# Rows in eight phases over 1024-row macro tiles, with the 31-tap convolution as block-Toeplitz matmuls

## The reference

```
mod = silu(c) @ w_ada + b_ada;  shift, scale, gate = split(mod, 3)
h = rmsnorm(x, norm_g) * (1 + scale) + shift
a_in, a_b, a_c, a_z, b_v, b_g, b_z = split(h @ w_in)          # 7 blocks of 512 columns
y_a = a_b * dwconv3(a_c * a_in) * silu(a_z)
u = dwconv31(b_v * sigmoid(b_g)) + conv_b_b
y_b = silu(head_layernorm(u, ln_g, ln_b)) * silu(b_z)         # norm over each head's 64 channels
x = x + gate * (concat([y_a, y_b]) @ w_out);  out = rmsnorm(x, final_g)
```

## Time and profile before

| | |
|---|---|
| time, median of 3 runs | 2577.07 us (2572.67 to 2577.63) |
| span of the profiled execution (slowest core) | 2570.0 us; all cores 2563.3 to 2570.0 |
| TensorE | busy 94% of the span |
| VectorE, ScalarE, GpSimd | busy 48%, 48%, 30% |
| DMA | 283 MB, 110 GB/s |
| TensorE's granted clock | 0.99 of full speed |

### The profile page before, as it was taken

The page is one execution under the profiler, slowest core; times in us unless marked ns, Lnnn a source line. Parts: engine busy times, 40 slices in busy tenths (PEclk is TensorE's granted clock), DMA queues, the critical chain, the costliest instruction groups (busy, mean ns, idle before and its releaser), DMA issues.

```text
span 2570.0 us, 46749 instructions; the slowest of 8 cores (2563.3 to 2570.0 us)
## 1 busy us (share of the span) xinstructions
PE 2428.4 (94%) x14724; PEld 1074.0 (42%) x14724; DVE 1245.8 (48%) x1972; ACT 1231.0 (48%) x2054; POOL 781.0 (30%) x838
## 2 busy tenths in 40 slices
PE   5799999999999999999999999999999999999995
PEld 1334444444444444444444444444444444444432
DVE  1234454545454545454545455455455455445455
ACT  1144555544555554455554455554454554455544
POOL 3113333223323223323323323323323323333314
PEclk9899999999999999999999999999999999999998
DMA  9954223344322344322334322344422334432232
GB/s 220 200 134 125 87 81 92 117 125 125 96 80 91 109 125 125 107 78 83 109 125 133 118 70 88 101 133 125 125 82 82 102 118 125 125 94 80 61 110 99
DMA packets 89914, 283.05 MB, mean 110 GB/s; under 512 B 15016, under 2 KB 24400, under 8 KB 89680
## 3 DMA queue, kind: packets, MB, share of 16 engines
q1 hardware_dynamic: 80176, 270.64, 35.0%
q0 software_dynamic: 9504, 9.44, 2.7%
HBM read 168.96 MB, written 67.13 MB: 92 GB/s over the span
## 4 chain that ended last, share of the span: by engine, by line
PE 70%; ACT 15%; issue 6%; POOL 3%; DMA 3%; DVE 2%; another core or an unknown queue 0%; ACTq 0%; SPq 0%; POOLq 0%; DVEq 0%
PE pb L446 50%; PE pb L646 12%; PE pb L575 6%; ACT L605 3%; ACT L609 3%; ACT tp L607 3%; POOL yT L619 2%; ACT tp L615 2%; DMA w_in_sb<-w_in 2%; PE pb L586 1%; ACT tp L608 1%; ACT gb L553 1%; ACT sq L580 1%; ACT tp L465 1%; DVE tp L563 0%
## 5 line engine op out<-in xcount | busy, mean ns | idle before, releaser
L446 PE MATMUL pb<-hT,w_in_sb 128*128 128x512 bf16 x7168 | 1594.7, 381 | 18.7 <-DMA w_in_sb<-w_in 16.7
L446 PEld LDWEIGHTS pb<-hT,w_in_sb 128*128 128x128 bf16 x7168 | 699.4, 98 | 860.8 <-issue 50.8
L646 PE MATMUL pb<-w_out_sb,yT 128*128 128x512 bf16 x2048 | 470.7, 380 | 17.4 <-POOL yT L619 16.6
L465 ACT ACTIVATE tp<-pb 128x512 f32<-128x512 f32 x384 | 225.1, 595 | 488.5 <-PE pb L446 487.8
L619 POOL TENSOR_TENSOR yT<-tp,gb 128x512 bf16<-128x512 f32 x128 | 145.1, 1155 | 862.1 <-ACT tp L615 862.1
L658 POOL TENSOR_TENSOR xb<-tp,xb 128x512 f32<-128x512 f32 x256 | 321.7, 1267 | 142.0 <-DVE tp L656 123.8
L693 ACT ACTIVATE tp<-xb 128x1024 bf16<-128x1024 f32 x128 | 135.3, 1057 | 428.9 <-POOL xb L658 428.9
L646 PEld LDWEIGHTS pb<-w_out_sb,yT 128*128 128x128 bf16 x2048 | 195.5, 98 | 247.6 <-issue 37.5
L703 DVE SCALAR_TENSOR_TENSOR xb<-xb,rsE,fg_bc 128x1024 f32<-128x1024 f32 x128 | 164.4, 1284 | 227.1 <-POOL rsE L701 227.1
L575 PE MATMUL pb<-V,WC 128*32 128x512 bf16 x4096 | 244.4, 381 | 0.0
L656 DVE TENSOR_TENSOR tp<-pb,gate_bc 128x512 f32<-128x512 f32 x256 | 173.7, 689 | 121.5 <-PE pb L646 109.8
(11 more groups left out here) (74 smaller groups left out, 1503.7 us busy)
## 6 DMA issues: line engine op xcount, KB each, us to landing
xb<-x SPq DMA_DIRECT2D x256, 512.0 KB, 6.4
y<-xb SPq DMA_DIRECT2D x128, 512.0 KB, 2.7
V<-u SPq DMA_DIRECT2D x128, 135.9 KB, 2.6
V<-u SPq DMA_DIRECT2D x128, 135.8 KB, 2.6
V<-u SPq DMA_DIRECT2D x128, 135.6 KB, 2.7
xb<-w_ada SPq DMA_DIRECT2D x24, 512.0 KB, 9.7
w_in_sb<-w_in POOLq DMA_DIRECT2D x14, 512.0 KB, 28.3
gate_bc<-gate_scratch SPq DMA_DIRECT2D x5, 512.0 KB, 7.2
```

The source lines that it names most:

```text
L446: T.op("tensor", lambda e, bank=bank, kc=kc: e.matmul(bank[:], lhsT=w_in_sb[:, kc, col0:col0 + 128], rhs=hT[:, kc, :], start=(kc == 0), st ...
L465: T.op("scalar", lambda e: e.activation(out=t[:], in_=bank[:], func=func, scale=scale), reads=[bkey], writes=[tkey])
L646: T.op("tensor", lambda e, kc=kc: e.matmul(bank[:], lhsT=yT[:, kc, sub * 128:(sub + 1) * 128], rhs=w_out_sb[:, kc, h * NT:(h + 1) * NT], s ...
```

## The change

A macro tile is 1024 consecutive rows, 16 per core. Its rows are dealt into eight phases r = 0 to 7: row 8n + r is column n of phase r. A tile is now half a macro tile: four phases of 128 rows each (q = 0 or 1), so that x is loaded and y stored with a stride of eight rows.

- **Convolution.** `V` now has 16 channels by 8 phases on the partitions and the index n on the free axis, 32 groups of 16 channels. `u` reaches it through a scratch tensor in HBM: `u_store` (4 transfers per tile, 131 KB, runs of 256 bytes) and `v_load` (4 per macro tile, 262 KB, runs of 256 bytes). One group's 31 taps are five matmuls of 128 by 128 with a block-Toeplitz matrix `wc` (SH = 5 shifts of n); the output has rows on the partitions and (phase, channel) on the free axis. A macro tile needs 8 `conv` of 20 matmuls with 128 columns each. The Toeplitz matrices are built at the start (`wc_build`, 8 instructions of 128x2560 and 8 stores of 655 KB) and are loaded again for each macro tile, 655 KB per `conv`, into a ring of two buffers (`wc_load`).
- **Head norm.** The 64 channels of a head now lie on the free axis: VectorE adds the bias and sums them (`s1`, `s2`, `s4`), ScalarE squares (`s3`), GpSimd takes the power and multiplies (`s4`, `s5`). The steps are handed out one per `tick()`, which each projection group and each `conv` calls. The result is turned back by a crossbar DMA on SP (`s6`, 262 KB, 4 per macro tile), then ScalarE's Silu and a VectorE multiply into `gb` (`fin_half`). No Ln or Exp is left.
- **Norm of x.** The 32 TensorE transposes per tile go away (except for tile 0): `xbar` turns `xs` by crossbar DMA, 4 of 262 KB per tile, and ScalarE applies the modulation in place in one of two `hT` buffers (`h_mod`, 8 per tile). The scaling moves from GpSimd to ScalarE.
- **Seams.** The rows right of each macro tile that isn't its sequence's last (11 times 16 rows) are projected once at the start (`halo_pairs`, 128 matmuls with 176 columns). PSUM is now one ring of 8 banks instead of 6 and 2; the ring of x buffers has 6 instead of 8.

```diff
-UW = 544
-TAP0 = (0, 1, 8, 9, 16, 17, 24, 25)
+PH = 8
+MT = 1024
+SH = 5
...
-        V = sb("V", [128, 4, 4, UW], BF16)
...
+        WC = Ring("wc", [sb("wc%d" % i, [128, 4 * SH * 128], BF16) for i in range(2)], T)
+        V = sb("V", [128, 32, 132], BF16)
...
+        def xbar(i, sub):
+            hT = hTb[i % 2]
+            T.dma("sync", lambda e: e.dma_start_transpose(out=hT[:, :, sub * 128:(sub + 1) * 128], in_=xs[:, sub, :]),
+                  reads=[("xs", sub)], writes=[("hTs", i % 2, sub)], semkey=("xt", i % 2, sub))
...
+        def h_mod(i, kc, eng="scalar"):
+            hT, s = hTb[i % 2], mac_seq[i // 2]
+            r, w = [("hTs", i % 2, sub) for sub in range(4)] + ["gsT", "shT"], [("hT", i % 2, kc)]
+            if eng == "scalar":
+                T.op("scalar", lambda e: e.activation(out=hT[:, kc, :], in_=hT[:, kc, :], func=AF.Identity, scale=gsT[:, kc, s:s + 1],
+                                                      bias=shT[:, kc, s:s + 1]), reads=r, writes=w)
...
+        def wc_load(h):
+            w, wkey = WC.next(pin=True)
+            T.dma("sync", lambda e: e.dma_start(out=w[:], in_=wc_d[h]), reads=[("wcd", h)], writes=[wkey], semkey=("wcl", wkey[1]))
+            wc_slot[h] = (w, wkey)
...
+        def u_store(i, j):
+            m, q = divmod(i, 2)
+            T.dma("sync", lambda e: e.dma_start(out=u_d[m % 2, j * 128:(j + 1) * 128, 4 * q:4 * q + 4, :],
+                                                in_=u_sb[:, j, :].rearrange("p (s n) -> p s n", s=4)),
+                  reads=[("u", j)], writes=[("ud", m % 2, q, j)], semkey=("us", q, j))
...
+        def v_load(m, j):
+            T.dma("sync", lambda e: e.dma_start(out=V[:, 8 * j:8 * j + 8, 2:130],
+                                                in_=u_d[m % 2, j * 128:(j + 1) * 128].rearrange("(g c) s n -> (c s) g n", c=16)),
+                  reads=[("ud", m % 2, 0, j), ("ud", m % 2, 1, j)], writes=[("V", j)], semkey=("vl", j))
...
+        def tick():
+            for st_ in list(lnq):
+                if st_[0]() is None:
+                    st_.pop(0)
+                if not st_:
+                    lnq.remove(st_)
...
+        def conv(m, h):
+            tick()
+            j = h // 2
+            bank, bkey = PB.next(pin=True)
+            w, wkey = wc_slot.pop(h)
+            for g in range(4):
+                for k in range(SH):
+                    T.op("tensor", lambda e, g=g, k=k: e.matmul(
+                        bank[:, g * 128:(g + 1) * 128], lhsT=V[:, 4 * h + g, k:k + 128], rhs=w[:, (g * SH + k) * 128:(g * SH + k + 1) * 128],
+                        start=(k == 0), stop=(k == SH - 1)),
+                        reads=[wkey, ("V", j), "Vl", "Vr"], writes=[bkey], signal=(g == 3 and k == SH - 1))
+            WC.unpin(wkey)
...
+            def s1():
+                T.op("vector", lambda e: e.tensor_tensor(out=o4, in0=bank[:].rearrange("p (g r c) -> p r g c", g=4, r=PH), in1=cb, op=ALU.add),
+                     reads=[bkey, "cbb"], writes=[okey])
+                PB.unpin(bkey)
+
+            def s2():
+                T.op("vector", lambda e: e.reduce_sum(out=ls[:, 0, :], in_=o3, axis=mybir.AxisListType.X), reads=[okey], writes=[lskey])
+                T.op("vector", lambda e: e.tensor_scalar(out=ls[:, 1, :], in0=ls[:, 0, :], scalar1=1.0 / 64, scalar2=None, op0=ALU.mult),
+                     reads=[lskey], writes=[lskey])
+                T.op("vector", lambda e: e.tensor_tensor(out=o3, in0=o3, in1=bc(1), op=ALU.subtract), reads=[okey, lskey], writes=[okey])
+
+            def s3():
+                sq[0], sqkey[0] = SQ.next(pin=True)
+                T.op("scalar", lambda e: e.activation(out=sq[0][:], in_=o[:], func=AF.Square), reads=[okey], writes=[sqkey[0]])
+
+            def s4():
+                T.op("vector", lambda e: e.reduce_sum(out=ls[:, 2, :], in_=sq[0][:].rearrange("p (r c) -> p r c", r=PH), axis=mybir.AxisListType.X),
+                     reads=[sqkey[0], lskey], writes=[lskey])
+                SQ.unpin(sqkey[0])
+                T.op("vector", lambda e: e.tensor_scalar(out=ls[:, 2, :], in0=ls[:, 2, :], scalar1=1.0 / 64, scalar2=LN_EPS, op0=ALU.mult, op1=ALU.add),
+                     reads=[lskey], writes=[lskey])
+                T.op("gpsimd", lambda e: e.tensor_tensor(out=ls[:, 3, :], in0=ls[:, 2, :], in1=mhalf[:], op=ALU.pow),
+                     reads=[lskey, "mhalf"], writes=[lskey])
+
+            def s5():
+                T.op("gpsimd", lambda e: e.tensor_tensor(out=xn[:, :, (h % 2) * 64:(h % 2) * 64 + 64], in0=o3, in1=bc(3), op=ALU.mult),
+                     reads=[okey, lskey], writes=[(xnkey, h % 2)] + ([xnkey] if h % 2 == 0 else []))
+                TP.unpin(okey)
+                LS.unpin(lskey)
+
...
+                def s6():
+                    if len(BR.pinned) == len(BR.bufs):
+                        return False
+                    got.extend(BR.next(pin=True))
+                    br, brkey = got
+                    T.dma("sync", lambda e: e.dma_start_transpose(out=br[:], in_=xn[:].rearrange("p r c -> p (r c)")),
+                          reads=[xnkey, (xnkey, 0), (xnkey, 1)], writes=[brkey], semkey=("yt", brkey[1]))
+                    XN.unpin(xnkey)
+                    return None
+
+                def fin_half(q):
+                    def f():
+                        if (m, q, j) not in zdone:
+                            return False
+                        br, brkey = got
+                        tt, ttkey = TP.next()
+                        T.op("scalar", lambda e: e.activation(out=tt[:], in_=br[:, 4 * q:4 * q + 4, :].rearrange("p r n -> p (r n)"), func=AF.Silu,
+                                                              scale=lng[:, j:j + 1], bias=lnb[:, j:j + 1]),
+                             reads=[brkey, "lng", "lnb"], writes=[ttkey])
+                        gv = gb[:, j, 4 * q:4 * q + 4, :].rearrange("p r n -> p (r n)")
+                        T.op("vector", lambda e: e.tensor_tensor(out=gv, in0=gv, in1=tt[:], op=ALU.mult),
+                             reads=[ttkey, ("gb", j, q)], writes=[("gb", j, q)])
+                        if q == 1:
...
+                steps += [s6, lambda: None, fin_half(0), fin_half(1)]
+            steps[0]()
+            lnq.append(steps[1:])
...
-        def conv_b(j):
-            bank, bkey = PB.next(pin=True)
-            for p in range(8):
-                for g in range(4):
-                    T.op("tensor", lambda e, p=p, g=g: e.matmul(
-                        bank[32 * g:32 * g + 32, :], lhsT=WC[:, (j * 4 + g) * 8 + p, :], rhs=V[:, g, j, TAP0[p]:TAP0[p] + NT],
-                        start=(p == 0), stop=(p == 7), tile_position=(0, 32 * g)),
-                        reads=[("WC", j)] + [("V", k, g) for k in range(4)], writes=[bkey], signal=(p == 7 and g == 3))
...
-        def conv_mean(j):
-            bank, bkey, vv, vkey = cst[j]
-            T.op("tensor", lambda e: e.matmul(bank[:], lhsT=Bn[:], rhs=vv[:], start=False, stop=True, skip_group_check=True),
...
+        for h in range(8):
+            wc_build(h)
+        pair_all("a2", 0)
+        for n in range(6):
+            a_next(1, n)
         for j in range(4):
             zb(0, j)
...
+        for kc in range(8):
+            h_mod(1, kc, "vector" if kc % 2 else "scalar")
...
+            if q == 1:
+                wc_load(0)
+                wc_load(1)
+                v_left(m)
...
+                    a_next(nxt, j)
+                if q == 1 and j:
+                    v_load(m, j - 1)
...
+            if pm >= 0:
+                out_proj(pm, q, conv_in=m if last else None)
...
+            if q == 0:
+                work = [lambda j=j: pair("a2", i, j) for j in range(4)] + [lambda j=j: zb(i, j) for j in range(4)]
+                for n, f in enumerate(work):
+                    f()
+                    if pm >= 0 and n < 4:
+                        conv_a(1, n)
+                    if fin and n in (0, 1):
+                        d_finish()
+                    if nxt is not None:
+                        h_mod(nxt, n)
+            else:
+                work = [f for j in range(4) for f in (lambda j=j: pair("a2", i, j), lambda j=j: zb(i, j))]
+                for n, f in enumerate(work):
+                    f()
+                    if fin and n in (0, 1):
+                        d_finish()
+                    if not last:
+                        conv(m, n)
+                        if n < 6:
+                            wc_load(n + 2)
+                    if nxt is not None:
+                        h_mod(nxt, n)
```

782 lines of the change are left out of this document (399 added, 383 removed).

## The result

The changed kernel takes 2648.37 us (median of 5 runs) against 2577.07, ratio **1.026** (95% interval 1.023 to 1.028): slower by 2.6%, where 2425 was forecast, and above the range's end of 2620. The profiled execution spans 2633.9 us.

What follows compares the result with a forecast made beforehand. TensorE's program order was taken as the bound: 126 + 35 + 10 + 2090 (its matmuls) + 113 + 14 + 15 + 15 = 2418 us of span, 2425 as median with 7 us added. Range of 8 in 10: 2285 to 2620 us.

Steps and rivals of the forecast that it cites:

- the a2 product of group 0 ends near 4.4 us into the stage: Start of the stage with conv: VectorE's a2 product ends at 4.4 us, and the first norm turn is issued at 19.
- two last norms with their waits 4.3: VectorE in the stage with conv: two last norms of output rows, 4.3 us, ahead of the first turn.
- the term of +7.5 us for the stage: Stage with conv: `conv` 7 ends at 37.2 instead of 29.7 us, in each of 15 macro tiles, 113 us.
- `conv` 7: Last conv of the stage: its weight load stands behind the second turn on SP, so it begins at 36.1 us.
- the loop: Norm in the stage with conv: turn, Silu, product, variance, power and GpSimd product lead to the next turn, 10.6 us.
- the next tile's last `h_mod`: Tile seam: it follows zb's own 0.6 us on ScalarE, +0.5 us at each of 31 seams, 15 in all.
- Short matmuls, reduction, power: Prices per instruction: 0.056 us per 128-column matmul on TensorE, 0.68 per VectorE reduction, 1.7 per GpSimd power.
- Rival D: TensorE's short matmuls take 97 ns each because weight loads aren't hidden, total 2530 us; chance 0.09.
- X + 6.6: Time from one norm turn to the next: X, the crossbar transfer, taken as 4 us, plus 6.6 us of other steps.
- rival C: Crossbar turns keep the 16 DMA engines busy, making the kernel slower; 2700 us at 8 us per turn; chance 0.21.
- The start: Before the steady part: +35 us for stores and the build of `wc`, +10 for tile 2's loads behind the gate.
- The end: From the last matmul to the kernel's end: stays at 15 us.

Runs made afterwards that it cites:

- f2: The change with the first half tile's 3-tap convolutions moved from ahead of out_proj to the next tile's glu phase, all work kept: 2602.52 us.
- f1: The change without the final norm of output rows finished in stages with conv, and with the Silu halves two slots later; work left out: 2495.51 us.
- e1: The change with y stores issued behind the conv weight loads of h=2 and 3 in SyncE's order, same work: 2630.94 us.
- e3: The change without the conv weight loads of h=2 to 7 in every stage; output not the reference's: 2646.71 us.
- e7: The change without the weight loads of h=2 to 7, with Silu halves two slots later and the output finish cut in two: 2605.56 us.
- f7: The change with 3-tap convolutions moved, Silu halves later, start and end reordered and y stores later, all work kept: 2529.56 us, ratio 0.981 to the kernel before.
- e5: The change with the two Silu halves of a turned norm output two slots later in ScalarE's order, same work: 2595.16 us.
- e9: The change with the last three row finishes of a stage with conv moved behind groups 1, 3 and 5, same work: 2698.21 us.
- e2: The change with all conv weight loads issued from ScalarE's queue instead of SyncE's, same work: 2706.45 us.

## Why the prediction was wrong

The span is 2633.9 instead of 2418: 216 us. From the trace, the first stage starts at 237.2, where the sum had 126 + 45 + 27.6 of matmuls + 5 = 203.6: 34 us. The 14 macro tiles from there take 2121.3 us, where 14 x 141.9 = 1986.6 were forecast: **135 us**, 9.6 each. The rest, to the end, takes 275.4 instead of 228: 48 us.

- **The step that failed** is "the a2 product of group 0 ends near 4.4 us into the stage", and with it "two last norms with their waits 4.3". I let VectorE and ScalarE enter the stage without backlog. The product ends 9.9 us in, and four last norms stand in the stage, with 8.8 us of waits. The first turn is issued at 25.1, not at 19. In the sum this is the term of +7.5 us for the stage: up to the next tile's eighth matmul the forecast is 29.7 + 7.5 + 0.5 + 1.5 (seven matmuls) = 39.2 us, and 47.8 were measured. Where no row finish stands in the stage, the first turn is at 18.9 and the stage lasts 41.0 (first stage of f2), or 18.6 and 39.0 (f1). That these come near the forecast is in part chance: the forecast held two last norms and these stages none, and their a2 product still ends 2.5 to 2.7 us after the forecast's.
- **What is late next** was named in part. For `conv` 7 I had its weights: they land at 1039.8 and it begins at 1040.1, 41.3 us in instead of 36.1. In the first stage, `conv` 5 waits 11.1 us for its weights behind the first turn, as the loop had it. What I hadn't are the wait ahead of h = 2, behind the y stores, and 3.1 us instead of 0.5 for the next tile's last `h_mod`. e1, e3 and e7 show that which of these waits appears has little bearing on the time.
- **Short matmuls, reduction, power: right.** Twenty of 128 columns take 1.28 us, the reduction 0.68, the power 1.65. Rival D falls. So does the Trainium skill's figure of about 81 ns for a matmul with its weight load ("TensorE: Matmul & The Clock Gate", "Back-to-back issue gap"): here it is 56.
- **The loop: right in its sum, partly by luck.** A round takes 10.5 us, as X + 6.6 gave with X = 4. But the turn lands 3.1 us after its issue, and the rest takes 7.4; two errors of 0.9 and 0.8 cancel. I had left out ScalarE's Square (0.61), and GpSimd's product takes 1.51 instead of 1.16.
- **The turns' transfers.** The DMA queue is busy for 50%: rival C falls, and the kernel is slower without its mechanism. By the Trainium skill's 1309 ns for each 128 x 128 ("VectorE: DVE Perf Modes", "The three transpose paths") a turn would be an estimated 10.5 us in series. By the Trainium skill's 261 GB/s ("DMA: Bandwidth & Descriptors", "Latency and other measured facts") it would be an estimated 1.0 us. The trace's 3.1 lies between them.
- **The clock** was not in the sum: granted 0.934 over the span against 0.99 before. In the 14 macro tiles TensorE is busy for 138.3 us each instead of 133.4, and idle for 13.2 instead of 8.5. By the trace it works for 8.9 us of each macro tile at half clock, which is 4.4 us of work lost; what of them falls within the stage costs no time of its own, as e3 shows.
- **The start** was mis-sized: +79 instead of +45 on the slowest core, +72 on the mean of the cores. The build of `wc` holds back tile 1's products on VectorE; moved away, it holds back SyncE, then the buffers. On the mean of the cores no run here took out more than 9 of these us, so how much of the start it explains stays open.
- **The end**: 33 us from the last matmul to the end instead of 15, since x loads of the last four rows stand behind four y stores. Loading two of them earlier leaves 27 (f7). The other 30 us of the last stretch hold one more stage with its 9; the 20 that are left were not tried apart.

What is shown for the steady part: it is not the weight loads (e1, e3, e7), and what stands in VectorE's queue ahead of the norm sets how long the stage is (f2 with all of the work, its first stage above all; f1 as a bound). The shares are 2.5 us a stage for the 3-tap convolutions and 6.2 for the four row finishes. The turn in the loop is worth 2.6 more, but the forecast had it. The shares don't sum to the 9.6 exactly, and how GpSimd's adds and powers and ScalarE's Squares divide the rest stays open: no run made either faster.

## What to carry to other kernels

An engine that is half idle on the mean may still enter a stage late; follow its queue from the phase before, and count all that stands in it with its waits. When a wait is taken away and the time stays, look where it went: the length of the stage, not the name of the wait, tells the bound. To move an engine's work out of the phase ahead of its tight stage (f2, 46 us) can be worth as much as to mend a loop in it (e5, 53 us).

## What the runs showed that I had not expected

After an idle time of 7 us TensorE's next twenty short matmuls ran at the half clock, in 2.29 instead of 1.28 us, and so did about four of the eight large ones behind them. Without weight loads (e3), where 12 us of idle time came at the seam with a few matmuls between, the stage's clock was 0.87 instead of 0.92, and the time was the same. A row finish whose own work on VectorE is 1.4 us lengthened a round of the norm's loop by 3 us when it was put inside (e9). A turn of 262 KB landed after 4.9 us instead of 3.1 where another queue's weight load ran beside it (e2).
